# Linear attention and its borders: weight splits behind two borders, value rows between key decays, key turns before the row wait, half of the scaling on ScalarE

## The chip, the cores and the metric

The kernel runs on one core of a Trainium2 chip. The metric is the device time of one execution in microseconds (us); lower is better.

## What is computed

Two transformer blocks in float32 on 512 tokens of width 1024. The first (dilated attention, a convolution, a mixture of 32 experts) is untouched. The second prepends 16 meta tokens (528 rows) and computes

```
proj = rmsnorm(h) @ w_in            # stick-breaking q,k,v; linear q,k,v; gate rows g_r; gate rank g_lr; merge gates
sb   = stick_breaking(sb_q, sb_k, sb_v)                       # 8 heads of 64
glog = log_sigmoid(g_lr @ w_gk_up + b_gk) / 16
# gated linear attention, 4 heads, keys of 128, values of 256:
S_t  = diag(exp(glog_t)) S_{t-1} + k_t^T v_t ;  o_t = q_t S_t
o    = rmsnorm(o, gla_head_norm) * silu(g_r)
mix  = (sigmoid(m_sb) * (sb @ w_sb_out) + sigmoid(m_gla) * (o @ w_gla_out)) @ w_o
h    = h + rmsnorm(mix)
ffn  = (gelu(dwconv(rmsnorm(h) @ w_up)) * (rmsnorm(h) @ w_gate)) @ w_down
h    = h + rmsnorm(ffn)
```

## The kernel before, in words

Each stage is a block of its own, written out by hand for each engine with semaphores between them; at the end of a block all engines meet at a barrier. The order of the work on each engine is the order of the code. The stages that matter here are stick_breaking (until 1058 us), gated_linear (until 1251), mix_and_project (until 1518) and feed_forward.

**Weights in two parts.** A product of float32 is made of three products of fp32r parts (function three, L1670 to L1672). So each weight piece of 128 x 1024 is split: ScalarE copies it into a high part (Parts.high, L1561), VectorE subtracts that from the raw values to give the low part (Parts.low, L1569), and TensorE waits for the low one (Parts.use). There are four places for split pieces and three for raw chunks; the DMA queue loads chunk c when the last piece of chunk c - 3 has its low part (Parts.load_until, L1525). Pieces are numbered and split in order: low_ok and high_ok count them. GK_AT + 2 is piece 19, the third key head of the linear attention; the next block's first pieces are split in the block before. UP_AT + 2 and UP_AT + 3 are the second column tile's pieces of the feed-forward.

**gated_linear.** First the gate rank (two products, pieces LR_AT), whose results ScalarE takes (L2376), then eight small products with the gate's weights (L2279) into three PSUM banks in turn, each freed by a take; then keys. Then the seven levels of a binary scheme for the attention inside a chunk (L2297), with products of value rows between them: 20 of them (four column blocks by five row tiles), 24 matmuls each, again three banks. A row tile 4 (the 16 meta rows) is the last that reads a column block's weights, and behind its take ScalarE splits the pieces that take their places. After the last level VectorE decays the queries (L2509), ScalarE computes the key decays in 4 heads x 5 spans (L2415), VectorE multiplies the keys (L2511).

**The chunk loop.** Five chunks: the 16 meta tokens and four of 128. In each, TensorE turns the decayed keys (4 transposes, L2334), waits for the state and for the rows of the chunk before, forms the outputs (L2342 and L2344: attention times values, queries times state, banks 1 and 2), the new state's product (L2349), and one product of gate rows (bank 7); then it waits for the normed rows and turns them (8 transposes, L2365). ScalarE takes the keys (L2429), sums four heads' squares (L2434), takes the root (L2437), the gate rows (L2440), splits a piece in odd chunks, and takes the turned rows (L2424). VectorE updates the state (L2524), forms the variance (L2531), its inverse (L2533), and scales four heads from PSUM into rows (L2537).

**mix_and_project** ends with the second norm, whose rows are turned (L2681), taken by ScalarE (L2769) and given low parts by VectorE (L2854).

Of the kernel before, what the change touches and what calls it, by code (L numbers as in the profile page):

```python
# [14 lines left out]
P = 128  # L15
# [1837 lines left out]
def stick_breaking(g):  # L1853
# [27 lines left out]
    with ExitStack() as cx:  # L1881
# [132 lines left out]
        @block.scalar  # L2014
        def _(act):
            def take_projection(n):
                first, m, half = outputs[n]
                act.wait_ge(ready, n + 1)
                bank = psum[:, BANKS[n % 8], :]
                lo, width = columns_of(first, half)  # L2020
                for r in range(2):
                    src, h = bank[HD * r:HD * r + HD, :], 2 * m + r
                    if first == Q_AT:
                        for d in range(2):
                            last = act.activation(q2[HD * d:HD * d + HD, h, lo:lo + width], src[:, 0:width], ACT.Copy, scale=HD ** -0.5)
                    elif half == 0:
                        act.activation(k2[h][HD:, 0:META], src[:, 0:META], ACT.Copy)
                        last = act.activation(k2[h][0:HD, 0:2 * P], src[:, META:LATER_KEYS], ACT.Copy)
                    else:
                        last = act.activation(k2[h][HD:, META:], src[:, 0:2 * P], ACT.Copy)  # L2030
                last.then_inc(taken, 1)
                if half == 1:
                    parts.high(act, first + m + W_SLOTS)

            def take_rows(r):
                c, t = row_outputs[r]
                n = len(outputs) + r
                act.wait_ge(ready, n + 1)
                if t == TT:
                    act.wait_ge(zeroed, 1)  # L2040
                rows = P if t < TT else META
                act.activation(v[0:rows, t, c * 256:(c + 1) * 256], psum[0:rows, row_bank(n), 0:256], ACT.Copy).then_inc(taken, 1)

            for n in range(len(outputs)):
                take_projection(n)
            step = Steps(act, astep)

            def log_term(h):

                act.wait_ge(z_sb, 6 * h + 6)  # L2050
                if h >= 2:
                    act.wait_ge(w_ok, 2 * (h - 1))
                z, t = zbuf[:, h % 3, :], sbuf[:, h % 2, :]
                step(act.activation(t, z, ACT.Abs))
                step(act.activation(t, t, ACT.Exp, scale=-1.0))
                act.activation(t, t, ACT.Ln, bias=1.0).then_inc(soft, 1)

            def weights(h):
                z, t = zbuf[:, h % 3, :], sbuf[:, h % 2, :]
                act.wait_ge(arg_ok, 6 * h + 4)  # L2060
                act.activation(z[:, 0:Z_META], t[:, 0:Z_META], ACT.Exp).then_inc(w_ok, 1)
                act.wait_ge(arg_ok, 6 * h + 6)
                act.activation(z[0:META, Z_META:], t[0:META, Z_META:], ACT.Exp).then_inc(w_ok, 1)

            def take(h):
                lo = 64 * (h % 2)
                act.wait_ge(pv_ps, 3 * h + 2)
                act.activation(sbT[lo:lo + 64, h // 2, META:], psum[0:HD, 5, :], ACT.Copy).then_inc(pv_sb, 1)
                act.wait_ge(pv_ps, 3 * h + 3)
                act.wait_ge(q_ps, h + 1)  # L2070
                act.activation(sbT[lo:lo + 64, h // 2, 0:META], psum[0:HD, 6, 0:META], ACT.Copy).then_inc(pv_sb, 1)
                act.activation(gq[:, h // 2, (h % 2) * HALF:(h % 2 + 1) * HALF], psum[:, 6, META:META + HALF], ACT.Copy,
                               scale=DK ** -0.5).then_inc(q_sb, 1)

            act.wait_ge(zeroed, 2)
            log_term(0)
            take_rows(0)
            take_rows(1)
            log_term(1)
            for r in range(2, TT + 1):  # L2080
                take_rows(r)
            parts.high(act, GQ_AT)
            take_rows(TT + 1)
            parts.high(act, GQ_AT + 1)
            for r in range(TT + 2, 2 * (TT + 1)):
                take_rows(r)
            parts.high(act, GQ_AT + 2)
            parts.high(act, GQ_AT + 3)
            for h in range(HEADS):
                weights(h)  # L2090
                if h + 2 < HEADS:
                    log_term(h + 2)
                take(h)
                if h % 2:
                    parts.high(act, GQ_AT + h // 2 + W_SLOTS)

        @block.vector
        def _(dve):
# [74 lines left out]
                elif h % 2 == 0:  # L2173
                    parts.low(dve, GQ_AT + h // 2 - 1 + W_SLOTS)
            add_other_keys(HEADS - 1)
            parts.low(dve, GK_AT + 2)

        @block.sync
        def _(sp):
# [4 lines left out]
def gated_linear(g):  # L2184
# [55 lines left out]
    with ExitStack() as cx:  # L2240
# [9 lines left out]
        o_ps, s_ps, s_ok = sem("out_in_psum"), sem("state_in_psum"), sem("state_ready")  # L2250
        sq, var, root = sem("out_squares"), sem("out_variance"), sem("out_root")
        rows_ok, oT_ps, oT_ok = sem("out_rows_ready"), sem("oT_in_psum"), sem("oT_ready")
        block = cx.enter_context(nc.Block())

        @block.gpsimd
# [9 lines left out]
        def _(pe):  # L2265
# [60 lines left out]
            pe.wait_ge(lv_ok, LEVELS + 1)  # L2326

            pe.wait_ge(dec, 1)
            for c, (c0, n) in enumerate(span):
                vt = v[0:n, (c - 1) % (TT + 1), :]  # L2330
                for h in range(GH):
                    if c and h == 0:
                        pe.wait_ge(kd_sb, c)
                    last = pe.transpose(psum[0:n, 0, h * P:(h + 1) * P], k[:, h, c0:c0 + n], ident)  # L2334
                last.then_inc(kd_ps, 1)
                if c:
                    pe.wait_ge(s_ok, 2 * c)
                    pe.wait_ge(rows_ok, c)
                for h in range(GH):
                    at_ = attm[:, h, :] if c == 0 else att[:, h, c0 - META:c0 - META + P]  # L2340
                    dst = psum[0:n, 1 + h // 2, (h % 2) * DV:(h % 2 + 1) * DV]
# [15 lines left out]
                turned(pe, psum[:, 7, 0:width], w, x, lo, width).then_inc(gr_ps, 1)  # L2357
                if c % 2:
                    parts.read_by(GR_AT + c // 2, gr_ps, c + 1)
                pe.wait_ge(rows_ok, c + 1)  # L2360
                for half in range(2):
                    if c:
                        pe.wait_ge(oT_ok, 2 * (c - 1) + half + 1)
# [6 lines left out]
        def _(act):  # L2370
# [7 lines left out]
            half = lambda x, h, i: x[:, h, i * HALF:(i + 1) * HALF]  # L2378
            for i in range(2):
                take(LR + i, lrT[:, i * HALF:(i + 1) * HALF], 16, HALF)  # L2380
            parts.high(act, LR_AT + W_SLOTS)
            act.wait_ge(nb_ok, 1)
            for h in range(GH):
# [12 lines left out]
            def take_value_rows(r):  # L2396
                c, t = row_outputs[r]
                rows_ = P if t < TT else META
                take(ROWS + r, v[0:rows_, t, c * 256:(c + 1) * 256], rows_, 256)
                if t == TT:  # L2400
                    parts.high(act, GV_AT + 2 * c + W_SLOTS)
                    parts.high(act, GV_AT + 2 * c + 1 + W_SLOTS)

            for n in range(LEVELS):
                act.wait_ge(diff, n + 1)
                act.activation(level_part(e, n), level_part(e, n), ACT.Exp, scale=1.0 / 16).then_inc(e_ok, 1)
                take_value_rows(2 * n)
                take_value_rows(2 * n + 1)

            act.wait_ge(qk_ok, LEVELS)  # L2410
            act.activation(flat(e), flat(cs), ACT.Exp, scale=-1.0 / 16).then_inc(qd_e, 1)
# [1 line left out]
            for h in range(GH):  # L2413
                for c, (c0, n) in enumerate(span):
                    last = act.activation(e[:, h, c0:c0 + n], cs[:, h, c0:c0 + n], ACT.Exp, scale=1.0 / 16, bias=nlast[:, h, c:c + 1])  # L2415
            last.then_inc(kd_e, 1)
            for r in range(2 * LEVELS, len(row_outputs)):
                take_value_rows(r)

            def take_oT(c):  # L2420
                c0, n = span[c]
# [5 lines left out]
            for c, (c0, n) in enumerate(span):  # L2427
# [7 lines left out]
                                   accum_out=ss[0:n, h:h + 1]).then_inc(sq, 1)  # L2435
                act.wait_ge(var, c + 1)
                act.activation(rstd[0:n, :], rstd[0:n, :], ACT.Sqrt).then_inc(root, 1)  # L2437
                act.wait_ge(gr_ps, c + 1)
                width = UP_PARTS[c % 2][1]
                act.activation(gr[:, c, 0:width], psum[:, 7, 0:width], ACT.Copy).then_inc(gr_sb, 1)  # L2440
# [5 lines left out]
        def _(dve):  # L2446
# [5 lines left out]
            for l in range(LEVELS):  # L2452
# [2 lines left out]
                step(dve.scalar_tensor_tensor(out=masks[:, l, :], in0=xor, scalar=1.0, in1=g["before"], op0=ALU.is_equal,  # L2455
                                              op1=ALU.mult))
            dve.engine_nop().then_inc(masks_ok, 1)
            parts.low(dve, LR_AT + W_SLOTS)

            dve.wait_ge(soft, 1)  # L2460
# [54 lines left out]
            for c, (c0, n) in enumerate(span):  # L2515
# [11 lines left out]
                        last.then_inc(s_ok, 1)  # L2527
                dve.wait_ge(sq, 4 * c + 4)
                if c:
                    dve.wait_ge(root, c)  # L2530
                dve.tensor_scalar(rstd[0:n, :], ss[0:n, :], 1.0 / DV, EPS, ALU.mult, ALU.add).then_inc(var, 1)  # L2531
                dve.wait_ge(root, c + 1)
                step(dve.reciprocal(rstd[0:n, :], rstd[0:n, :]))  # L2533
                if c:
                    dve.wait_ge(oT_ps, 2 * c)
                for h in range(GH):
                    last = dve.tensor_scalar(rows[0:n, h * DV:(h + 1) * DV], psum[0:n, 1 + h // 2, (h % 2) * DV:(h % 2 + 1) * DV],  # L2537
                                             rstd[0:n, h:h + 1], None, ALU.mult)
                last.then_inc(rows_ok, 1)
# [55 lines left out]
def mix_and_project(g):  # L2595
# [24 lines left out]
    with ExitStack() as cx:  # L2620
# [167 lines left out]
        def _(dve):  # L2788
# [67 lines left out]
            for t in range(TT + 1):  # L2856
# [5 lines left out]
                    parts.low(dve, UP_AT + 1)  # L2862
                if t:
                    low_rows(t - 1)
            parts.low(dve, UP_AT + 2)
            parts.low(dve, UP_AT + 3)
            low_rows(TT)

        @block.sync
        def _(sp):  # L2870
            sp.dma_start(gain, a["norm_mix_post_2"].to_broadcast([P, D])).then_inc(loads, 16)
            sp.dma_start(gpre, a["norm_ffn_pre_2"].to_broadcast([P, D])).then_inc(loads, 16)
            sp.dma_start(g["meta"][0:HISTORY, :], a["meta_tokens_2"][META - HISTORY:, :]).then_inc(loads, 16)
            parts.load_until(sp, 42)
    parts.new_phase()


def feed_forward(g):
# [15 lines left out]
    with ExitStack() as cx:  # L2894
# [96 lines left out]
        def _(dve):  # L2991
# [12 lines left out]
            def product(m):  # L3004
                dve.wait_ge(act_ok, m + 1)
                dve.wait_ge(ready, 3 * m + 3)
                dve.tensor_tensor(products[m], y[:, m % 2, :], psum[:, BANKS[(3 * m + 2) % 6], :], ALU.mult).then_inc(prod_ok, 1)  # L3007

            for m in range(FM):
                conv(m)  # L3010
                if m:
# [50 lines left out]
```

## Time and profile before

| | |
|---|---|
| time, median of 3 runs | 1889.44 us (1889.11 to 1890.83) |
| profiled execution, span from first to last instruction | 1896.1 us |
| TensorE (PE) busy | 1746.9 us, 92% |
| VectorE (DVE) busy | 799.2 us, 42% |
| ScalarE (ACT) busy | 587.5 us, 31% |
| mean granted TensorE clock | 0.972 of 2.4 GHz |
| DMA | 355.38 MB, mean 187 GB/s |

The span belongs to one execution and is 6.7 us longer than the median of the runs. Matmuls are pipelined, so the records of neighbouring ones overlap; an idle time of PE is counted from the end of the last record.

### The profile page before, as it was taken

To read this page: it belongs to the slowest core of one execution; us is meant where nothing else is said; L and a number is where in the kernel's file an instruction comes from. 1 tells how busy PE (TensorE), PEld (TensorE's weight loads), DVE (VectorE), ACT (ScalarE), POOL (GpSimd) and SP (SyncE) were. 2 spreads that over 40 slices of the span, in tenths; PEclk is the share of its full clock that TensorE was granted. 3 is DMA by queue.
4 is the path that set the end of the run, shared out by engine and by line. 5 is a ranking of instruction groups with operands and counts; after the bars stand their busy time and mean duration, and the time that the engine had idled before them with its cause. 6 is when DMAs were issued, how large, how long until landed. Compare 5 with 4: busy or idle time off the path is not lost. (4 is left out here: it accounts for less than half of the span.)

```text
span 1896.1 us, 27345 instructions
## 1 busy us (share of the span) xinstructions
PE 1746.9 (92%) x11698; PEld 1351.5 (71%) x11698; DVE 799.2 (42%) x1348; ACT 587.5 (31%) x992; POOL 61.3 (3%) x86
## 2 busy tenths in 40 slices
PE   6999989999989889938999899899999999999997
PEld 2883445666555556528965799789998789999886
DVE  3864556221111111144377567342246544444333
ACT  4333422100000000036677433443223423322322
POOL 1001000000000000020000000000000000000000
PEclk9999989999999999978999899999999999999999
DMA  9855623899999999971210111122223033223221
GB/s 370 272 184 163 263 104 137 334 427 426 426 428 428 426 426 427 426 281 51 76 36 9 46 45 45 45 87 92 90 90 111 1 113 99 89 89 99 103 88 45
DMA packets 111217, 355.38 MB, mean 187 GB/s; under 512 B 8663, under 2 KB 71405, under 8 KB 97399
## 3 DMA queue, kind: packets, MB, share of 16 engines
q1 hardware_dynamic: 106342, 343.89, 47.2%
q0 software_dynamic: 4224, 9.33, 1.4%
q8 instruction: 94, 1.54, 0.3%
q10 hardware_dynamic: 530, 0.40, 0.1%
q14 instruction: 27, 0.22, 0.0%
HBM read 330.21 MB, written 23.33 MB: 186 GB/s over the span
## 5 line engine op out<-in xcount | busy, mean ns | idle before, releaser
L1670 PE MATMUL psum<-parts_memory 128*128 128x256 f32 (+3 forms) x1136 | 347.3, 306 | 14.7 <-issue 4.7
L1671 PE MATMUL psum<-parts_memory 128*128 128x256 f32 (+3 forms) x1136 | 344.1, 303 | 0.0
L1672 PE MATMUL psum<-parts_memory 128*128 128x256 f32 (+3 forms) x1136 | 343.3, 302 | 0.0
L1569 DVE TENSOR_TENSOR parts_memory<-fixed,parts_memory 128x1024 fp32r<-128x1024 f32 x139 | 167.1, 1222 | 206.6 <-ACT parts_memory L1561 206.3
L1670 PEld LDWEIGHTS psum<-parts_memory 128*128 128x128 f32 x1136 | 218.8, 193 | 24.6 <-issue 8.1
L1672 PEld LDWEIGHTS psum<-parts_memory 128*128 128x128 f32 x1136 | 218.7, 193 | 6.9
L1671 PEld LDWEIGHTS psum<-parts_memory 128*128 128x128 f32 x1136 | 218.6, 192 | 6.9
L1670 PE MATMUL psum<-mix_parts,parts_memory 128*128 128x256 f32 (+2 forms) x664 | 206.4, 311 | 4.7 <-PEq L2620 4.0
L1671 PE MATMUL psum<-mix_parts,parts_memory 128*128 128x256 f32 (+2 forms) x664 | 207.4, 312 | 0.0
L1672 PE MATMUL psum<-mix_parts,parts_memory 128*128 128x256 f32 (+2 forms) x664 | 206.4, 311 | 0.0
L1561 ACT ACTIVATE parts_memory<-fixed 128x1024 fp32r<-128x1024 f32 x139 | 143.2, 1055 | 123.9 <-PE psum L1672 109.7
L1329 PE MATMUL psum<-fixed,first_block_memory 128*64 128x256 f32 x1216 | 138.0, 380 | 16.7 <-DMA fixed<-in_w_exp_up_dram 14.7
L1329 PEld LDWEIGHTS psum<-fixed,first_block_memory 128*64 128x64 f32 x1216 | 94.8, 137 | 65.2 <-issue 34.1
L1670 PEld LDWEIGHTS psum<-mix_parts,parts_memory 128*128 128x128 f32 x664 | 126.2, 190 | 12.6 <-issue 4.2
L1672 PEld LDWEIGHTS psum<-mix_parts,parts_memory 128*128 128x128 f32 x664 | 126.4, 190 | 7.0
L1671 PEld LDWEIGHTS psum<-mix_parts,parts_memory 128*128 128x128 f32 x664 | 125.9, 190 | 7.4
L1329 PE MATMUL psum<-attention_memory,first_block_memory 128*64 128x256 f32 x896 | 101.8, 380 | 13.7 <-DMA attention_memory<-in_w_exp_up_dram 11.0
L1329 PEld LDWEIGHTS psum<-attention_memory,first_block_memory 128*64 128x64 f32 x896 | 70.2, 137 | 49.5 <-issue 27.4
L1450 DVE TENSOR_TENSOR first_block_memory<-first_block_memory,psum 128x256 f32<-128x256 f32 x33 | 13.9, 422 | 216.2 <-PE psum L1329 216.2
L1395 ACT ACTIVATE first_block_memory<-psum 128x512 f32<-128x512 f32 x36 | 21.5, 596 | 223.6 <-PE psum L1313 223.6
L1313 PE MATMUL psum<-parts_memory 128*128 128x256 f32 x576 | 85.9, 294 | 1.4 <-DVE parts_memory L1433 1.4
L1313 PEld LDWEIGHTS psum<-parts_memory 128*128 128x128 f32 x576 | 72.6, 190 | 16.8 <-issue 12.3
(412 smaller groups left out, 2365.1 us busy)
## 6 DMA issues: line engine op xcount, KB each, us to landing
fixed<-in_w_exp_gate_dram SPq DMA_DIRECT2D x19, 2048.0 KB, 29.7
fixed<-in_w_exp_up_dram SPq DMA_DIRECT2D x19, 2048.0 KB, 30.9
fixed<-in_w_exp_down_dram SPq DMA_DIRECT2D x19, 2048.0 KB, 31.7
fixed<-in_w_in_dram SPq DMA_DIRECT2D x36, 1024.0 KB, 5.1
attention_memory<-in_w_exp_up_dram SPq DMA_DIRECT2D x14, 2048.0 KB, 31.0
attention_memory<-in_w_exp_down_dram SPq DMA_DIRECT2D x14, 2048.0 KB, 31.2
attention_memory<-in_w_exp_gate_dram SPq DMA_DIRECT2D x14, 2048.0 KB, 29.5
fixed<-in_w_mod_dram SPq DMA_DIRECT2D x8, 2048.0 KB, 8.8
```

The lines of the kernel that those rows point to most:

```text
L1313: last = pe.matmul(psum[:, bank, part * BC:part * BC + BC], h2P[:, i, t, (2 * u + part) * P:(2 * u + part + 1) * P], pick[:, t, :], start= ...
L1329: last = pe.matmul(psum[half(h), bank, 0:256], x[:, k, :], w[:, k, 256 * h:256 * h + 256], start=(k == 0), stop=(k == KT - 1))
L1395: act.activation(xT[:, i, 2 * u:2 * u + 2, :], psum[:, BX + u % 2, :].rearrange("p (k n) -> p k n", k=2), ACT.Copy).then_inc(xt_ok, 1)
L1450: dve.tensor_tensor(h, h, strided(psum[:, BU, 0:256], 4), ALU.mult).then_inc(h_ok, 1)
L1561: act.activation(out, raw, ACT.Copy).then_inc(self.high_ok, 1)
L1569: dve.tensor_tensor(out, raw, high.bitcast(F32), ALU.subtract).then_inc(self.low_ok, 1)
L1670: pe.matmul(out, x(0), w(0), start=start, stop=False)
L1671: pe.matmul(out, x(0), w(1), start=False, stop=False)
L1672: return pe.matmul(out, x(1), w(0), start=False, stop=stop)
```

## The change

- In stick_breaking the split of piece GK_AT + 2 is dropped, and made in gated_linear: its high part behind the two gate-rank takes, its low part behind the masks.
- The takes of value rows 14, 15 and 16 stand between the key decays of the heads; the splits that followed the takes come after all decays.
- In the chunk loop, the keys of chunk c + 1 are turned behind the gate rows of chunk c and before the wait for its rows. The wait for the rows ahead of the outputs goes, as the row turns have waited for them already.
- Heads 2 and 3 are scaled by ScalarE (semaphores out_inverse_root and out_rows_of_scalar_ready), heads 0 and 1 by VectorE.
- The low parts of UP_AT + 2 and UP_AT + 3 are made at the start of feed_forward; their high parts stay where they were. Two weight chunks that wait for them are issued there too.

```diff
@@ stick_breaking, scalar and vector
-                if h % 2:
+                if h % 2 and h + 1 < HEADS:
                     parts.high(act, GQ_AT + h // 2 + W_SLOTS)
             add_other_keys(HEADS - 1)
-            parts.low(dve, GK_AT + 2)
@@ gated_linear, tensor
+            def turn_keys(c):
+                c0, n = span[c]
+                if c:
+                    pe.wait_ge(kd_sb, c)
+                for h in range(GH):
+                    last = pe.transpose(psum[0:n, 0, h * P:(h + 1) * P], k[:, h, c0:c0 + n], ident)
+                last.then_inc(kd_ps, 1)
+
+            turn_keys(0)
             for c, (c0, n) in enumerate(span):
-                for h in range(GH):
-                    if c and h == 0:
-                        pe.wait_ge(kd_sb, c)
-                    last = pe.transpose(psum[0:n, 0, h * P:(h + 1) * P], k[:, h, c0:c0 + n], ident)
-                last.then_inc(kd_ps, 1)
                 if c:
                     pe.wait_ge(s_ok, 2 * c)
-                    pe.wait_ge(rows_ok, c)
...
+                if c < TT:
+                    turn_keys(c + 1)
                 pe.wait_ge(rows_ok, c + 1)
+                pe.wait_ge(rows_act, c + 1)
@@ gated_linear, scalar
                 take(LR + i, lrT[:, i * HALF:(i + 1) * HALF], 16, HALF)
+            parts.high(act, GK_AT + 2)
             parts.high(act, LR_AT + W_SLOTS)
...
                     last = act.activation(e[:, h, c0:c0 + n], cs[:, h, c0:c0 + n], ACT.Exp, scale=1.0 / 16, bias=nlast[:, h, c:c + 1])
+                if h < GH - 1:
+                    take_value_rows(2 * LEVELS + h)
             last.then_inc(kd_e, 1)
             for r in range(2 * LEVELS, len(row_outputs)):
-                take_value_rows(r)
+                if r >= 2 * LEVELS + GH - 1:
+                    take_value_rows(r)
+                if r >= 2 * LEVELS + GH - 2:
+                    for q in range(2 * LEVELS if r == 2 * LEVELS + GH - 2 else r, r + 1):
+                        split_after(q)
...
                 act.activation(rstd[0:n, :], rstd[0:n, :], ACT.Sqrt).then_inc(root, 1)
+                if c:
+                    act.wait_ge(oT_ps, 2 * c)
+                act.wait_ge(inverse, c + 1)
+                for h in range(GH - BY_ACT, GH):
+                    last = act.activation(rows[0:n, h * DV:(h + 1) * DV], psum[0:n, 1 + h // 2, (h % 2) * DV:(h % 2 + 1) * DV],
+                                          ACT.Copy, scale=rstd[0:n, h:h + 1])
+                last.then_inc(rows_act, 1)
@@ gated_linear, vector
+            parts.low(dve, GK_AT + 2)
             parts.low(dve, LR_AT + W_SLOTS)
...
-                    dve.wait_ge(root, c)
+                    dve.wait_ge(rows_act, c)
...
-                step(dve.reciprocal(rstd[0:n, :], rstd[0:n, :]))
+                dve.reciprocal(rstd[0:n, :], rstd[0:n, :]).then_inc(inverse, 1)
+                dve.wait_ge(inverse, c + 1)
...
-                for h in range(GH):
+                for h in range(GH - BY_ACT):
@@ mix_and_project, vector and sync
-            parts.low(dve, UP_AT + 2)
-            parts.low(dve, UP_AT + 3)
             low_rows(TT)
-            parts.load_until(sp, 42)
+            parts.load_until(sp, 40)
@@ feed_forward, vector
+            parts.low(dve, UP_AT + 2)
+            parts.low(dve, UP_AT + 3)
             for m in range(FM):
```

## Rows read from the trace of the kernel before

**Rows 1.** The page's first part: busy time, share of the span, instructions.

```profile
PE 1746.9 (92%) x11698; PEld 1351.5 (71%) x11698; DVE 799.2 (42%) x1348; ACT 587.5 (31%) x992; POOL 61.3 (3%) x86
```

**Rows 2.** TensorE's waits from 1200 to 1300 us: in total, times, longest.

```profile
PE psum L2365 <- DVE fixed L2537: 5.0, 4, 1.6
PE psum L1670 <- PEq L2240: 1.0, 1, 1.0
```

**Rows 3.** Timeline, border behind stick_breaking: start, duration, engine, what, [idle before <- releaser].

```profile
1055.19 0.69 DVE L2128 TENSOR_TENSOR fixed<-fixed,psum 64x512 f32<-64x512 f32 x1 [5.68 <-ACT fixed L2071]
...
1056.55 1.23 DVE L1569 TENSOR_TENSOR parts_memory<-fixed,parts_memory 128x1024 fp32r<-128x1024 f32 x1 [0.67 <-ACT parts_memory L1561]
...
1058.10 0.56 PE L1670 MATMUL psum<-parts_memory 128*128 128x264 f32 x1 [3.60 <-PEq L1881]
```

**Rows 4.** Timeline, ScalarE's split and the eight small gate products.

```profile
1066.91 1.04 ACT L1561 ACTIVATE parts_memory<-fixed 128x1024 fp32r<-128x1024 f32 x1
1067.06 4.26 PE L2279 MATMUL psum<-linear_memory 16*128 16x264 f32 x16 [0.47 <-ACT linear_memory L2376]
```

**Rows 5.** Timeline, key decays, the value row that waits, decayed keys, first key turns.

```profile
1182.19 5.58 ACT L2415 ACTIVATE linear_memory<-linear_memory,fixed 128x16 f32<-128x16 f32 x20 [7.21 <-DVE fixed L2509]
...
1187.80 2.36 DVE L2511 TENSOR_TENSOR linear_memory<-linear_memory 128x2112 f32<-128x2112 f32 x1 [5.64 <-ACT linear_memory L2415]
...
1188.09 0.39 PE L1670 MATMUL psum<-parts_memory 128*128 128x256 f32 x1 [2.74 <-ACT linear_memory L2376]
...
1197.35 0.60 PE L2334 MATMUL psum<-fixed,linear_memory 128*16 128x128 f32 x4 [0.46 <-ACT linear_memory L2376]
```

**Rows 6.** Timeline, a middle chunk of the loop.

```profile
1214.34 1.66 DVE L2524 SCALAR_TENSOR_TENSOR linear_memory<-linear_memory,fixed,psum 128x256 f32<-128x256 f32 x4 [7.59 <-PE psum L2349]
...
1216.57 1.66 DVE L2537 TENSOR_SCALAR fixed<-psum,fixed 128x256 f32<-128x256 f32 x4
...
1217.17 0.38 ACT L2440 ACTIVATE fixed<-psum 128x256 f32<-128x256 f32 x1 [0.85 <-PE psum L1672]
...
1218.28 1.09 PE L2365 MATMUL psum<-fixed 128*128 128x128 f32 x8 [1.14 <-DVE fixed L2537]
...
1219.21 0.60 PE L2334 MATMUL psum<-fixed,linear_memory 128*128 128x128 f32 x4
1219.65 0.60 PE L2342 MATMUL psum<-linear_memory 128*128 128x256 f32 x2
```

**Rows 7.** Timeline, the row turns of the last chunk.

```profile
1249.09 1.09 PE L2365 MATMUL psum<-fixed 128*128 128x128 f32 x8 [1.58 <-DVE fixed L2537]
```

**Rows 8.** Timeline, border behind mix_and_project.

```profile
1513.67 1.09 PE L2681 MATMUL psum<-fixed,mix_memory 128*128 128x128 f32 x8 [1.34 <-DVE mix_memory L2846]
1514.37 1.09 ACT L2769 ACTIVATE mix_parts<-psum 128x512 fp32r<-128x512 f32 x2 [1.29 <-PE psum L2681]
1514.73 2.35 DVE L1569 TENSOR_TENSOR parts_memory<-fixed,parts_memory 128x1024 fp32r<-128x1024 f32 x2
...
1517.00 1.28 DVE L2854 TENSOR_TENSOR mix_parts<-psum,mix_parts 128x512 fp32r<-128x512 f32 x2
...
1518.75 0.55 PE L1670 MATMUL psum<-mix_parts,parts_memory 128*128 128x256 f32 x1 [3.99 <-PEq L2620]
```

**Rows 9.** Windows: stretch, length, busy per engine; PEclk 1.00 is 2.4 GHz.

```profile
1186.37:1189.78 3.41, 1.69 (x14) 1.70 (x15) 1.98 (x1) 3.41 (x9) 0.00 (x0) 1.00 0.00 0
1247.81:1251.22 3.41, 1.14 (x9) 0.94 (x9) 2.35 (x5) 1.29 (x4) 0.00 (x0) 1.00 0.00 0
1251.22:1254.63 3.41, 3.41 (x16) 3.41 (x17) 1.66 (x5) 3.15 (x7) 0.00 (x0) 0.50 1.02 321
1517.46:1524.28 6.82, 5.53 (x26) 5.56 (x27) 0.82 (x2) 0.42 (x2) 0.00 (x0) 0.50 1.05 351
1056.66:1063.48 6.82, 5.38 (x24) 5.41 (x25) 5.76 (x15) 0.00 (x0) 2.42 (x4) 0.50 0.01 5
```

**Rows 10.** Windows: the chunk loop behind chunk 0's low clock.

```profile
1206.84:1250.18 43.34, 38.36 (x249) 34.86 (x248) 15.00 (x38) 18.38 (x56) 0.00 (x0) 1.00 0.00 1
```

More of the change, by code:

```diff
@@ L2252, in gated_linear @@
         rows_ok, oT_ps, oT_ok = sem("out_rows_ready"), sem("oT_in_psum"), sem("oT_ready")
+        rows_act, inverse = sem("out_rows_of_scalar_ready"), sem("out_inverse_root")
+        BY_ACT = 2
         block = cx.enter_context(nc.Block())
@@ L2399, in take_value_rows, with split_after @@
                 take(ROWS + r, v[0:rows_, t, c * 256:(c + 1) * 256], rows_, 256)
+            def split_after(r):
+                c, t = row_outputs[r]
                 if t == TT:
@@ L2406, in _ @@
                 act.activation(level_part(e, n), level_part(e, n), ACT.Exp, scale=1.0 / 16).then_inc(e_ok, 1)
-                take_value_rows(2 * n)
-                take_value_rows(2 * n + 1)
+                for r in (2 * n, 2 * n + 1):
+                    take_value_rows(r)
+                    split_after(r)
             act.wait_ge(qk_ok, LEVELS)
@@ L2415, in _ @@
                     last = act.activation(e[:, h, c0:c0 + n], cs[:, h, c0:c0 + n], ACT.Exp, scale=1.0 / 16, bias=nlast[:, h, c:c + 1])
+                if h < GH - 1:
+                    take_value_rows(2 * LEVELS + h)
             last.then_inc(kd_e, 1)
             for r in range(2 * LEVELS, len(row_outputs)):
-                take_value_rows(r)
+                if r >= 2 * LEVELS + GH - 1:
+                    take_value_rows(r)
+                if r >= 2 * LEVELS + GH - 2:
+                    for q in range(2 * LEVELS if r == 2 * LEVELS + GH - 2 else r, r + 1):
+                        split_after(q)
             def take_oT(c):
```

## The prediction

> **What bounds the kernel now.** I read the page first: TensorE is busy for 92% of the span [rows 1], the chain that ended last names its products and almost no wait, so the kernel goes at TensorE's pace and a change is worth what it takes out of TensorE's idle time or gives back of its clock. The list of TensorE's waits, taken over the linear attention, shows the wait of the row turns for VectorE: 5.0 us in four pieces [rows 2]. The timelines around the edits show four more places:
>
> - the border from stick-breaking to linear attention: TensorE starts at 1058.10 after 3.60 us idle. VectorE's add ends at 1055.88; what still runs is a weight split of ScalarE and then of VectorE, up to 1057.78. No one in that block reads it [rows 3];
> - the value rows: 2.74 us, ended by a take of ScalarE's that stood behind twenty key decays, 5.58 us from 1182.19 [rows 5];
> - the border from linear attention to mixing: 1.58 us before the last row turns [rows 7] and 1.0 behind them [rows 2];
> - the border from mixing to feed-forward: TensorE has stopped at 1514.76 (1513.67 and 1.09), VectorE makes two lows from 1514.73 to 1517.08 and only then the last token rows' low halves, to 1518.28; TensorE starts at 1518.75, 3.99 us [rows 8].
>
> The windows of the granted clock show that it fell to half (1.2 GHz) at or near three of these borders, and stayed at 2.4 GHz at the 2.74 us wait [rows 9].
>
> **Part by part.** The sum is made in the profiled execution, span 1896.1 us. The runs shown have a median of 1889.44 us, 6.7 us less; I subtract the same microseconds from the median.
>
> *First border.* High and low of piece 19 go behind the border. The barrier then waits for VectorE's add at 1055.88 in place of 1057.78: 1.90 us less idle [rows 3]. The DMA queue waits for nothing new, since the chunks issued in that block need earlier lows. What moves: ScalarE now makes two splits where it made one, between the gate-rank takes and the eight gate takes. One costs 1.04 us [rows 4]. TensorE can run three of its eight small products into free banks: the eight take 4.26 us, some 0.5 each, so about 1.5 us from 1067.06, to 1068.6. The first take, which frees a bank, starts when the split ends, at 1067.95; with a second one it would start at 1068.9 to 1069.0 and last some 0.4 (0.38 for such a take in [rows 6]). So TensorE loses 0.7 to 1.04; I take 0.9. The weights themselves are wanted only two products later, and VectorE's extra low lies beside these (1.23 in [rows 3]); if that cover were gone it would cost that. Net 1.0.
>
> *Value rows.* Three takes move between the key decays. The decays of a head last 5.58 / 4 = 1.40 us, so the first take comes at about 1183.6, and TensorE, which comes to its next product at 1185.35 (1188.09 less 2.74), finds its bank. The 2.74 us go [rows 5]. Three takes of 0.4 put the decayed keys 1.2 us later; VectorE then needs 2.36 us for them and is done near 1191.3, while TensorE has value rows until about 1194.2 (the key turns at 1197.35, less 0.46 idle and less 2.7). Hidden, with 2.8 us to spare. The last weights' highs still follow the last take, as before. Gain 2.7.
>
> *Chunk loop.* Before, in a middle chunk: the state update ends at 1216.00, then variance, root, inverse, then four scalings 1216.57 to 1218.23; the gate rows end at 1217.14 (1218.28 less 1.14); row turns 1218.28; key turns 1219.21; outputs 1219.65 [rows 6]. After, VectorE scales two heads, 0.83 us, to 1217.40. No row shows ScalarE reading PSUM with a column as scale; the nearest is its take of the gate rows, 0.38 us for the same 128x256 [rows 6]. Two make 0.76, to 1217.3. Bounds: 0 beyond VectorE's half, or 0.83 each (twice the take and VectorE's time doubled), to 1218.23, which is no gain; I take the row's 0.38. TensorE turns the next keys from 1217.14 for 0.44 (start of the outputs less start of the turns) to 1217.58: by then the rows are ready. The 1.14 us wait is filled, and the next chunk starts without key turns. Three chunks: 3.4. The last chunk has no keys to turn; its 1.58 us wait [rows 7] shrinks by two scalings, 0.83. Chunk 0 has no wait there and moves only the order. Behind ScalarE's two scalings stand the take of the gate rows, a split in odd chunks (1.05), the oT takes and the key take; the scalings fit into 0.85 us that it idles before the gate rows [rows 6]. If they didn't, the key take is next to be late, and the state products. Gain 4.2.
>
> *Last border.* The lows of UP_AT + 2 and + 3 go into the next block; the last rows' lows start when ScalarE's second half lets them: its take starts at 1514.37, VectorE about 0.6 later (as it is free at 1514.8), and ends near 1516.3. The barrier's 0.47 (1518.28 to 1518.75) stays: TensorE starts at 1516.75, 2.0 us earlier [rows 8]. The loads of two weight chunks wait for these lows and go with them, some 2 us later and behind the next block's load of its gain; they are not split before the second column tile. TensorE wants the moved lows for that tile too, two products (some 8 us, by 5.53 us of work in the 6.8 us behind 1517.46 [rows 9]) after its start; two lows take 2.35, so they are there by 1519.2. Gain 2.0.
>
> Idle time together: 1.0 + 2.7 + 4.2 + 2.0 = 9.9 us.
>
> *The clock.* TensorE was at half rate for 5.38 us of its work behind the first border, 3.41 behind the second, 5.53 behind the last [rows 9]; at full rate these would cost half: 2.7, 1.7 and 2.8 us. Before the falls it had idled 3.60 in one piece, 1.58 and 0.99 around the row turns, and 3.99 [rows 2, 3, 7, 8]. Afterwards the idle pieces are 1.7, then 0.75 and 1.0, then 1.34 and 2.0 around 1.09 of turns [rows 8]. The first two are no more idle than the stretch of the value rows that kept its clock with 1.69 busy in 3.41 us. The third isn't: I let it fall and recover sooner, 1.1 of 2.8. In this execution that is 2.7 + 1.7 + 1.1 = 5.5. Bounds 0 and 7.2. Where the falls sit against the work differs between executions, so I take 4.0.
>
> One rule speaks to this. The clock fell at 1251.22 after a stretch with 1.14 us of work in it and no idle piece over 1.6 us [rows 9]. The Trainium skill, TensorE: Matmul & The Clock Gate, section "Why this matters for your kernels", advises no idle gap over about 3 us between bursts, as if shorter ones were safe; by it alone all three borders would keep their speed, which is the rival of full speed below. The trace disagrees with it, unless the row turns count as idle.
>
> **Sum.** 9.9 + 4.0 = 13.9: 1889.4 - 13.9 = 1875.5 us. A difference of 3.8 us (0.2%) is about what a measurement of this kernel can tell from no change.
>
> **Rivals.**
> 1. *Full speed at every border.* 9.9 + 7.2 = 17.1 gives 1872.3. For: two of three idle pieces are halved. Against: the fall at 1251.22. Chance 0.15.
> 2. *The clock gives nothing back*, because it falls on the shorter gaps as well: 1879.5. For: 1.58 and 0.99 were enough once. Against: 1.69 of work in 3.41 was not. 0.18.
> 3. *ScalarE's half is late*: the scalings take up to 0.83 each, or the key take behind them slips. The row wait shrinks only by the key turns: 3 x 0.44 in place of 4.2, 2.9 lost: 1878.4. For: ScalarE also carries a split in odd chunks. Against: 0.85 idle just there. 0.15.
> 4. *The waits are handed on.* Some other engine ends the two blocks last (ScalarE or the queue), and the value rows' 2.74 turn into a wait for the decayed keys. Left are the 4.2, less the 0.9 in ScalarE's queue: 1886.1. For: 0.47 of the last barrier isn't VectorE's. Against: every other end in rows 3 and 8 is earlier. 0.07.
> 5. *Slower: the clock stays low through the chunk loop.* Chunk 0 enters it at half speed already, and more turns stand together now. The loop's 43.3 us at full clock [rows 10] would cost up to 21.7 more: 1897.3. It decides from 28 us of work at half speed (13.9 twice); with 15 us or less the kernel is still over 6 faster. Against: with idle pieces in it the loop held full clock. 0.03.
>
> My forecast has the other 0.42. Faster by over 0.2% (under 1885.7): the forecast, rivals 1 to 3, 0.90; within 0.2%, rival 4, 0.07; slower 0.03. Range: from below full speed, 1871, to a late ScalarE without clock, 1879.5 + 2.9 = 1882.5. The likeliest alone: 1873.5 to 1877.5.
>
> **What would show it.** TensorE's idle before L1670 about 1.7 at the first border and 2.0 at the last; no wait of over 0.3 before the row turns of the middle chunks and about 0.75 in the last; no 2.7 before the value rows; the middle chunks over 1 us closer together; small gate products some 0.9 longer. The clock's falls behind the first two borders gone. The span near 1882. It is wrong if ScalarE's scalings take over 0.6 each, if a new wait for keys_ready stands before the state products, or if half-speed stretches turn up elsewhere.

## The result and the profile after

The changed kernel took 1881.66 us in the median of four runs (1879.37 to 1883.22), the kernel before 1890.13 in four runs beside it (1889.11 to 1892.60). The ratio is 0.9943, 95% interval 0.9926 to 0.9960: 10.8 us faster, from 7.6 to 14. It is an estimate of its own and not the quotient of the two medians, which lie 8.5 us apart. Both are given below where they differ. The forecast was 13.9 us faster and 1875.5, range 1871.0 to 1882.5; the median lies in the range, near its upper end. Two more series of the same kernel on other occasions gave 0.9919 and 0.9945, medians 12.8 and 13.1 us apart (below).

The profiled executions differ by more, spans 1896.1 and 1877.3. The stage windows of the changed kernel show where; they are cut at the end of the last product of stick-breaking, the first small gate product, the first level product, the first output product, the last row turn, and the last turn of the second norm. Columns: stretch, length, busy time of TensorE, its weight loads, VectorE, ScalarE, GpSimd, then the granted clock, the DMA share and GB/s.

```profile
1052.37:1060.64 8.27, 6.10 (x49) 5.92 (x49) 6.38 (x19) 1.86 (x6) 2.43 (x4) 1.00 0.02 4
1060.64:1092.53 31.89, 30.75 (x208) 28.90 (x209) 17.57 (x34) 18.38 (x26) 0.00 (x0) 0.89 0.22 67
1092.53:1189.40 96.87, 93.47 (x780) 89.51 (x780) 64.69 (x74) 36.78 (x57) 0.00 (x0) 1.00 0.11 34
1189.40:1235.81 46.41, 45.53 (x281) 40.37 (x280) 16.60 (x38) 26.99 (x79) 0.00 (x0) 0.96 0.14 45
1235.81:1498.86 263.05, 257.57 (x1937) 245.81 (x1936) 115.88 (x193) 95.50 (x180) 0.00 (x0) 1.00 0.26 85
1498.86:1877.28 378.42, 363.64 (x2089) 320.36 (x2088) 162.00 (x201) 110.34 (x174) 0.00 (x0) 0.99 0.28 91
```

The same six windows of the kernel before:

```profile
1054.50:1067.06 12.56, 8.49 (x49) 8.31 (x49) 9.04 (x25) 2.81 (x7) 2.42 (x4) 0.73 0.01 3
1067.06:1098.02 30.96, 30.48 (x208) 28.91 (x208) 15.01 (x27) 17.49 (x25) 0.00 (x0) 0.89 0.21 69
1098.02:1197.88 99.86, 93.72 (x780) 89.55 (x780) 64.70 (x74) 36.98 (x57) 0.00 (x0) 1.00 0.13 43
1197.88:1250.17 52.29, 47.31 (x281) 41.48 (x280) 20.53 (x48) 23.51 (x69) 0.00 (x0) 0.93 0.07 21
1250.17:1514.76 264.59, 259.11 (x1937) 247.35 (x1936) 116.02 (x194) 95.65 (x180) 0.00 (x0) 0.99 0.26 84
1514.76:1896.10 381.34, 364.55 (x2089) 321.31 (x2088) 161.87 (x201) 110.36 (x174) 0.00 (x0) 0.98 0.27 90
```

Line by line the change is -4.29, +0.93, -2.99, -5.88, -1.54, -2.92: 16.7 us. The other 2.1 of the 18.8 lie ahead of the first edit, where the code is the same (1054.50 against 1052.37). So two traces can differ by a few us there without any edit. Over all 13 traces of this case the first cut lies between 1048.00 and 1055.45 us, always behind the same code, and TensorE's clock was at half for 51 us ahead of it in the earliest and for 72 us in the latest: this is where much of the scatter of the spans comes from. The time from the first cut to the end is the better measure of an edit: 841.6 and 841.4 us in two traces of the kernel before, 824.9, 825.0 and 825.6 in three of the changed one.

In TensorE's waits of the changed kernel the 2.7 before the value rows and the row waits of the middle chunks are gone; these are the waits of 1040 to 1190 and of 1190 to 1300:

```profile
PE psum L1670 <- PEq L1881: 1.7, 1, 1.7
...
PE psum L2280 <- ACT fixed L2383: 0.7, 1, 0.7
...
PE psum L1670 <- PEq L2239: 1.0, 1, 1.0
PE psum L2372 <- DVE fixed L2564: 0.9, 1, 0.9
```

The timeline of a middle chunk, beside [rows 6]:

```profile
1206.49 0.88 DVE L2564 TENSOR_SCALAR fixed<-psum,fixed 128x256 f32<-128x256 f32 x2
1206.55 0.84 ACT L2460 ACTIVATE fixed<-psum,fixed 128x256 f32<-128x256 f32 x2 [0.31 <-DVE fixed L2559]
1206.88 0.60 PE L2335 MATMUL psum<-fixed,linear_memory 128*128 128x128 f32 x4
1207.27 0.39 ACT L2465 ACTIVATE fixed<-psum 128x256 f32<-128x256 f32 x1
1207.48 1.06 PE L2372 MATMUL psum<-fixed 128*128 128x128 f32 x8
...
1216.44 0.60 PE L2335 MATMUL psum<-fixed,linear_memory 128*128 128x128 f32 x4
```

ScalarE and VectorE scale two heads each side by side and end within 0.02 us of each other, at 1207.38. The key turns run meanwhile, and the row turns start at 1207.48 with no idle time ahead. The key turns of neighbouring chunks start 9.56 us apart (1206.88 to 1216.44); before it was 10.7.

The first border and the small gate products, beside [rows 3] and [rows 4]:

```profile
1054.07 0.36 PE L1670 MATMUL psum<-parts_memory 128*128 128x264 f32 x1 [1.71 <-PEq L1881]
...
1060.49 1.99 ACT L1561 ACTIVATE parts_memory<-fixed 128x1024 fp32r<-128x1024 f32 x2
...
1060.64 1.60 PE L2280 MATMUL psum<-linear_memory 16*128 16x264 f32 x6 [0.47 <-ACT linear_memory L2383]
...
1062.39 2.62 ACT L2383 ACTIVATE fixed<-psum,fixed 128x264 f32<-128x264 f32 x6
1062.90 3.13 PE L2280 MATMUL psum<-linear_memory 16*128 16x264 f32 x10 [0.66 <-ACT fixed L2383]
```

TensorE makes three products (six instructions), then waits 0.66 us for the take that stands behind two splits.

The last border, beside [rows 8]: the low halves start at 1499.09, TensorE at 1500.85, and the two moved lows lie behind it.

```profile
1499.09 1.29 DVE L2881 TENSOR_TENSOR mix_parts<-psum,mix_parts 128x512 fp32r<-128x512 f32 x2 [0.18 <-ACT mix_parts L2796]
...
1500.70 1.23 DVE L1569 TENSOR_TENSOR parts_memory<-fixed,parts_memory 128x1024 fp32r<-128x1024 f32 x1 [0.32 <-PEq L2647]
...
1500.85 0.35 PE L1670 MATMUL psum<-mix_parts,parts_memory 128*128 128x256 f32 x1 [1.99 <-PEq L2647]
```

### The profile page after: what moved, and what is told of

It is laid out like the page before. It is cut to its first block and busy times, and to the rows that moved or that the text cites. A ratio compares the mean times of both kernels' runs of the same rounds, so it can differ in the third digit from the quotient of the medians.

```text
span 1877.3 us, 27345 instructions
## 1 busy us (share of the span) xinstructions
PE 1741.2 (93%) x11698; PEld 1346.3 (72%) x11698; DVE 794.9 (42%) x1338; ACT 590.3 (31%) x1002; POOL 60.4 (3%) x86
## 3 DMA queue, kind: packets, MB, share of 16 engines
q8 instruction: 94, 1.54, 0.3%
## 5 line engine op out<-in xcount | busy, mean ns | idle before, releaser
L1670 PEld LDWEIGHTS psum<-parts_memory 128*128 128x128 f32 x1136 | 216.5, 191 | 19.4 <-issue 10.8
L1450 DVE TENSOR_TENSOR first_block_memory<-first_block_memory,psum 128x256 f32<-128x256 f32 x33 | 13.9, 422 | 214.6 <-PE psum L1329 214.6
L1313 PEld LDWEIGHTS psum<-parts_memory 128*128 128x128 f32 x576 | 72.6, 190 | 16.7 <-issue 12.3
```

The lines of the kernel that those rows point to most:

```text
L1313: last = pe.matmul(psum[:, bank, part * BC:part * BC + BC], h2P[:, i, t, (2 * u + part) * P:(2 * u + part + 1) * P], pick[:, t, :], start= ...
L1450: dve.tensor_tensor(h, h, strided(psum[:, BU, 0:256], 4), ALU.mult).then_inc(h_ok, 1)
L1670: pe.matmul(out, x(0), w(0), start=start, stop=False)
```

## The experiments

The idle terms can be read off; open were the clock's share, and why the timed runs showed 8.5 us between medians where the traces showed 18.8. Where a text below names a half-speed stretch, it is one in which the granted clock was 0.50, that is 1.2 GHz.

**1. The kernel before, unchanged.**

> The kernel before, unchanged, profiled once more and timed. Theory 1 (the profiled execution of before was a slow one, with more half-speed stretches around the edits than most): the new span lies near 1888 us, and at least one of the falls of the granted clock at the borders behind stick-breaking, linear attention and mixing is missing, shorter, or elsewhere. Theory 2 (those falls belong to every execution of before, and the change's clock gain was lost again elsewhere): span 1894 to 1897 with the same three falls, and the timed runs still 6 us shorter.

Ratio 1.0001 (0.9992 to 1.0010). On this occasion the unchanged kernel had a median of 1893.16 us in 33 runs that spread from 1887.69 to 1898.05: a median of four can be off by some us. The new span is 1891.3. Its stages before and behind the value rows:

```profile
1049.83:1061.52 11.69, 7.62 (x48) 7.44 (x49) 8.96 (x25) 2.81 (x7) 2.42 (x4) 0.85 0.01 4
...
1090.90:1192.28 101.38, 95.24 (x781) 91.06 (x781) 64.71 (x74) 36.97 (x57) 0.00 (x0) 0.98 0.14 42
```

Here the clock's low stretch behind the first border was shorter (11.69 against 12.56 us), but it fell at the 2.7 us wait of the value rows, where the first trace had none (101.38 against 99.86). From the first cut to the end both traces take the same, 841.4 and 841.6 us; they differ ahead of it, 1049.8 against 1054.5. Neither theory fits fully: the falls do move between executions, as theory 1 says, yet from the first cut on the first trace was not a slow one; its slow part was upstream. In both traces the kernel before loses to the clock at some of its waits, and not at the same ones.

**2. The first border's edit alone.**

```diff
-                if h % 2:
+                if h % 2 and h + 1 < HEADS:
                     parts.high(act, GQ_AT + h // 2 + W_SLOTS)
...
-            parts.low(dve, GK_AT + 2)        # stick_breaking
+            parts.high(act, GK_AT + 2)       # gated_linear, behind the gate-rank takes
+            parts.low(dve, GK_AT + 2)        # gated_linear, behind the masks
```

> Only the split of piece 19 moved behind the first border. Both theories: TensorE idles 1.7 us there instead of 3.6, the eight small gate products lose 0.7 to 1.0, net idle gain 1.0. Theory 1 (clock gives on average nothing much): 0 to 2 us faster. Theory 2 (the clock no longer falls behind this border, 2.7 us each time): 3 to 4 us faster.

Ratio 0.9997 (0.9986 to 1.0007): 0.6 us, from 2.6 faster to 1.3 slower. In the trace the wait at the border is 1.7 us and the small gate products wait 0.7 for a take. The clock did not fall at the border, but it fell at the untouched value-row wait. That agrees with theory 1; theory 2's 3 to 4 us lie outside the interval.

**3. The value rows' edit alone.**

```diff
                     last = act.activation(e[:, h, c0:c0 + n], cs[:, h, c0:c0 + n], ACT.Exp, scale=1.0 / 16, bias=nlast[:, h, c:c + 1])
+                if h < GH - 1:
+                    take_value_rows(2 * LEVELS + h)
...
```

> Only the three takes of value rows moved between the key decays. Both theories: the 2.74 us wait of TensorE disappears and the key turns start 2.7 to 3.0 us earlier against the last level, 2.7 us faster. Rival: a new wait for the decayed keys stands before the key turns and takes over 1 us of it back.

Ratio 0.9987 (0.9976 to 0.9998), 2.5 us. The stage of the levels takes 96.85 us, as in the changed kernel (96.87), against 99.86 and 101.38 before. No wait for the decayed keys took its place; the rival falls.

**4. The last border's edit alone.**

```diff
-            parts.low(dve, UP_AT + 2)        # mix_and_project
-            parts.low(dve, UP_AT + 3)
...
-            parts.load_until(sp, 42)
+            parts.load_until(sp, 40)
...
+            parts.low(dve, UP_AT + 2)        # feed_forward
+            parts.low(dve, UP_AT + 3)
             for m in range(FM):
```

> Only the two lows moved behind the border to the feed-forward. Both theories: TensorE idles 2.0 us there instead of 4.0. Theory 1: the clock still falls behind the border in most executions (the row turns with their gaps are enough), 2.0 us faster, up to 3. Theory 2: the clock stays up, 4 to 5 us faster. Rival: the second column tile of the feed-forward waits for the moved loads or lows, and there is no gain.

Ratio 0.9989 (0.9979 to 1.0000), 2.1 us. The last stretch takes 378.20 us against 381.34 and 381.03 before, 3 us less. The clock still fell behind the border, but for 3.41 us in place of 6.83:

```profile
1517.74:1521.15 3.41, 3.02 (x14) 3.06 (x15) 2.36 (x2) 0.39 (x1) 0.00 (x0) 0.50 0.50 169
1521.15:1524.57 3.42, 3.42 (x31) 3.42 (x31) 1.48 (x3) 1.34 (x2) 0.00 (x0) 1.00 1.01 334
```

That is theory 1: 2.0 of idle time and up to one more. The moved loads and lows cost nothing that the stretch shows.

**5. The changed kernel again, and 6. the chunk loop's two edits alone.**

> The changed kernel unchanged, timed in more runs. Theory 1 (the gain is the idle time taken out, 9.9 us, plus a clock gain of a few us that shows only over many executions): 10 to 14 us under the kernel before. Theory 2 (the clock gives nothing on average): 8.5 to 10 us. If the first comparison's 8.5 us between medians was mostly luck of four runs each, the ratio here lies under 0.9945.

Ratio 0.9919 (0.9899 to 0.9939), 11.5 to 19 us faster; the medians, 1879.57 and 1892.36, are 12.8 apart, which is theory 1's size. Theory 2's 8.5 to 10 lie below the interval. The trace takes 825.0 us from the first cut on, with the same falls as the first one.

```diff
-                    pe.wait_ge(rows_ok, c)            # ahead of the outputs
...
+                if c < TT:
+                    turn_keys(c + 1)
                 pe.wait_ge(rows_ok, c + 1)
+                pe.wait_ge(rows_act, c + 1)
...
+                for h in range(GH - BY_ACT, GH):      # ScalarE
+                    last = act.activation(rows[...], psum[...], ACT.Copy, scale=rstd[0:n, h:h + 1])
...
-                for h in range(GH):                   # VectorE
+                for h in range(GH - BY_ACT):
```

> Only the chunk loop's two edits, keys turned ahead and half of the scaling on ScalarE. Theory 1: the middle chunks lose their 1.1 us wait and get 1.1 to 1.3 us shorter each, the last wait goes from 1.6 to about 0.8; 4.2 to 4.7 us faster, and up to 1 more where the clock stays up at the border behind. Rival: ScalarE's scalings are late or push the key take back, the gain is 1.3 us.

Ratio 0.9985 (0.9976 to 0.9994), 2.8 us. In the trace the loop takes 48.07 us against 52.29, with the same half-speed stretch in chunk 0: 4.2 us, the forecast's term. The timed interval (1.1 to 4.5) includes it. The clock did not fall at the border behind the loop either: the stretch to the next cut takes 263.06 us against 264.59.

**7. Keys turned ahead, all scaling on VectorE.** The edit is the TensorE part of the diff above (turn_keys moved, the wait ahead of the outputs gone), without the wait for rows_act.

> Only the keys turned ahead of the row wait, all four scalings on VectorE. TensorE's wait before the row turns falls from 1.14 to about 0.7 in the middle chunks (0.44 of turns fill it), and stays 1.6 in the last. The chunks come 0.44 us closer together each. Rival: the wait stays 1.1, because the chain through VectorE starts with the outputs and not with the turns, so that the whole chunk moves up: also 0.44 each, but with other waits.

One execution, span 1891.0, with no timed series. The row turns wait:

```profile
1215.47 1.09 PE L2370 MATMUL psum<-fixed 128*128 128x128 f32 x8 [0.73 <-DVE fixed L2542]
1225.72 1.09 PE L2370 MATMUL psum<-fixed 128*128 128x128 f32 x8 [0.67 <-DVE fixed L2542]
1235.97 1.09 PE L2370 MATMUL psum<-fixed 128*128 128x128 f32 x8 [0.69 <-DVE fixed L2542]
1244.97 0.33 PE L2370 MATMUL psum<-fixed 128*128 128x128 f32 x1 [1.57 <-DVE fixed L2542]
```

0.7 in the middle chunks and 1.57 in the last, and 10.25 us from chunk to chunk, 0.44 less than 10.69. The loop takes 50.99 us. So of its 4.2 us the key turns give 1.3 and ScalarE's half 2.9: the latter takes some 0.7 more in each middle chunk and 0.7 in the last. One thing speaks against the prediction's reasoning on the clock: the waits around the last row turns are as long as before (1.57 and 0.99), and yet the clock stayed at 2.4 GHz behind them in this trace, where it fell in the five other traces with these waits.

```profile
1247.05:1253.88 6.83, 6.83 (x58) 6.83 (x59) 4.66 (x12) 6.52 (x15) 0.00 (x0) 1.00 0.96 308
```

**8. The changed kernel without the first border's edit.** Experiment 2's diff taken back.

> The changed kernel with the split of piece 19 back in the stick-breaking block. The single parts, timed alone, add up to 8.0 us, the whole to 12.8 to 15.3. Theory 1 (the parts are additive, the difference is noise of the timed runs): this is slower than the whole by the 3.4 us that the first border's two stages gained net in the trace (4.3 less 0.9), and the chunk loop stays at 46.4 us with 3.4 us of half clock. Theory 2 (the first edit also sets where the clock's falls sit against the later work): the chunk loop is back at 48.1 us with 6.8 us of half clock, and the whole difference is about 5 us.

Ratio 0.9942 (0.9921 to 0.9964), median 1881.81 against 1881.58 for the changed kernel on the same occasion: no difference that the timed runs can tell, though with some 4 us to either side on each they can't rule out 3.4 us. The first two stages, in its windows:

```profile
1054.92:1065.09 10.17, 6.10 (x49) 5.92 (x49) 7.61 (x20) 2.81 (x7) 2.43 (x4) 1.00 0.01 3
1065.09:1096.18 31.09, 30.61 (x209) 28.68 (x209) 16.43 (x33) 17.48 (x25) 0.00 (x0) 0.89 0.22 69
```

With 3.6 us of idle time the clock this time stayed up at the border. The two stages take 41.26 us against 40.16 in the changed kernel: with the clock alike in both, the edit gives 1.90 and costs 0.80. Theory 2 falls: the chunk loop stays at 46.4 us, so the shorter low stretch there isn't this edit's doing. Theory 1 has the loop right and not the 3.4 us: in this trace, from the first cut to the end, it is 0.5 us slower (825.4 against 824.9).

**9. The changed kernel once more.**

> The changed kernel once more, as the partner of the next one on the same chip: 12 to 16 us under the kernel before, and a span with the same falls of the clock behind the first gate products, in chunk 0 and behind the last border.

Ratio 0.9945 (0.9924 to 0.9965), 6.6 to 14 us faster; by the ratio 10.4 us, less than the 12 to 16 that I expected, by the medians (1881.58 and 1894.63) 13.1, within them. Span 1877.7; the falls are where the first trace of it has them, with one more, of 3.4 us, in the mixing stage (264.0 us instead of 263.05).

**10 and 11. Both splits behind the eight gate takes.** The improved version, run on two occasions:

```diff
                 take(LR + i, lrT[:, i * HALF:(i + 1) * HALF], 16, HALF)
-            parts.high(act, GK_AT + 2)
-            parts.high(act, LR_AT + W_SLOTS)
             act.wait_ge(nb_ok, 1)
             for h in range(GH):
                 for i in range(2):
                     take(LR + 2 + 2 * h + i, half(qe, h, i), P, HALF, scale=-1.0, func=ACT.Identity, bias=nbias[:, h:h + 1])
+            parts.high(act, GK_AT + 2)
+            parts.high(act, LR_AT + W_SLOTS)
```

> The changed kernel with both of ScalarE's splits moved behind the eight gate takes. If the 0.7 to 1.1 us that the small gate products lost come from the second split ahead of their takes, the wait before L2280 goes, the stage gets 0.7 to 1.1 us shorter than in the changed kernel and the time falls by as much. Rival: the products are slow by the half clock alone, and nothing changes; or the low parts come late and the third key head waits.

> The changed kernel with ScalarE's two splits behind the eight gate takes, again. If the 2.5 us that the stage of the gate products gained in the first trace (31.9 to 29.4) hold, this is 2 to 3 us faster than the changed kernel on the same chip. If only the 0.7 us wait belongs to the edit and the rest was the place of the clock's fall in one execution, under 1.5 us.

Ratios to the kernel before 0.9911 (0.9896 to 0.9926) and 0.9911 (0.9890 to 0.9931), medians 1876.63 and 1876.80, where the changed kernel had 1879.57 and 1881.58. ScalarE's takes now follow the products at once, and the splits come behind:

```profile
1060.38 0.38 ACT L2383 ACTIVATE linear_memory<-psum 16x264 f32<-16x264 f32 x1 [2.53 <-PE psum L1672]
1061.62 3.54 ACT L2383 ACTIVATE fixed<-psum,fixed 128x264 f32<-128x264 f32 x8 [0.86 <-PE psum L2280]
1065.06 2.00 ACT L1561 ACTIVATE parts_memory<-fixed 128x1024 fp32r<-128x1024 f32 x2
```

The window of that stage, the first of the two traces:

```profile
1060.82:1090.23 29.41, 28.93 (x208) 27.68 (x208) 17.50 (x34) 18.22 (x26) 0.00 (x0) 0.94 0.19 59
```

29.41 us in both traces against 31.89, 31.88 and 31.92 in three of the changed kernel: 0.7 is the wait, the rest a half-speed stretch that is 3.4 us long instead of 6.8. Whether the edit shortens that stretch isn't shown: in the second trace of the kernel before it is 3.4 us as well (29.38 us for the stage, with one split ahead of the takes). The third key head does not wait. The first expectation had the wait right and missed the size, 2.5 us in place of 0.7 to 1.1; in the second the stage's 2.5 held. From the first cut on the two traces take 822.0 and 822.3 us, some 3 less than those of the changed kernel. By the medians the timed runs are 2.9 and 4.8 us faster than the changed kernel's; the intervals of the ratios overlap with that one's, so the timed runs alone don't settle it.

## Why the prediction was right, and where it was off

- **First border, net 1.0.** Right: 1.90 less idle, 0.80 to 0.93 lost by the small gate products. Experiments 8 and 10 show both sides. The loss was avoidable: with the splits behind the takes nothing waited for them.
- **Value rows, 2.7.** 3.0 in the trace. The recorded wait leaves out the overlap of neighbouring matmuls: in an unbroken row records of 0.28 us start 0.12 apart, and the one behind the wait took 0.39. That is the missing 0.3.
- **Chunk loop, 4.2.** Right to 0.1. The price taken for ScalarE's scaling, 0.38 each from its take, was a little low: two last 0.84 where a sum of two takes is 0.76 and two pipelined ones less. It sits beside VectorE's 0.88 (I took 0.83), so nothing followed. Experiment 7 separates the two edits: 1.3 and 2.9.
- **Last border, 2.0.** Right: 3.99 became 1.99; the moved loads and lows were never waited for.
- **The clock, 4.0.** This is the term that was mis-sized. With the idle terms as measured (1.0 + 3.0 + 4.2 + 2.0 = 10.2) the first comparison leaves nothing for it by the medians and 0.6 by the ratio; the second series leaves 2.6 and 5.1, the third 2.9 and 0.2. In the first pair of traces it was 6.5 (16.7 less 10.2): 2.4 at the first border, 1.5 behind the linear attention, 0.9 at the last border, and 1.7 in chunk 0, which I hadn't forecast. That part, 52.29 to 46.41 less the loop's 4.2, shows in every trace with both the value rows' and the loop's edits and in none with one of them. Why is open; a kernel with those two alone wasn't run. The forecast priced the falls of one trace and scaled them down by a guess; the table below shows what the other traces say.
- **The row and the rule.** The clock fell behind idle pieces of under 2 us each, at the second border of the kernel before (1.58 and 0.99) and at the last border of the changed one (1.34 and 1.99), and it stayed up through 3.60 us in two traces (experiments 7 and 8). The Trainium skill, in TensorE: Matmul & The Clock Gate, section "Why this matters for your kernels", advises no gap over about 3 us; as a line between falls and no falls that disagrees with these traces on both sides.
- **Rivals.** Full speed at every border: the last border fell in each trace. ScalarE late: refuted by 0.84 beside 0.88. Waits handed on: no such wait, save the 0.66 that was priced. Slow chunk loop: its clock is 0.96 against 0.93 before. No clock gain: not excluded by the timed intervals of the first and third series, excluded by that of the second (11.5 to 19) and by the traces. The price of rival 5 was wrong: at half clock TensorE's 38.4 us of work in those 43.3 [rows 10] would take up to 38.4 us more, and not 21.7.
- **Luck.** The range was met with 0.8 us to spare, and not for the reason that its upper end was set for: ScalarE was not late. The forecast stood on a base of three runs, 1889.44, and the kernel before had medians of 1893.16, 1892.36 and 1894.63 on later occasions. As a difference, 13.9 lies above the first ratio's 10.8 and the third's 10.4 and below the second's 15.3.

The half-speed stretches behind each place, in the 13 traces, sorted by the wait that stands there:

| place | with the wait of before | with it shortened or gone |
|---|---|---|
| first border, 3.60 us or 1.71 | 6.8 us in three traces, 3.4 in two, none in two | none in six |
| value rows, 2.74 or none | 3.4 in three, none in three | none in seven |
| behind the linear attention, 1.58 or 0.86 | 3.4 in five, none in one | none in seven |
| last border, 3.99 or 1.99 | 6.8 in six | 3.4 in seven |

With the edits the falls were gone at three places and shorter at the last in every trace; without them three of the four came only in some executions. The value rows' fall, which the forecast put at nothing, belongs in the sum. An estimate from these counts and the stage lengths (2.4 us lost to a stretch of 6.8 us at the first border, 1.5 to each of 3.4, and 0.9 at the last border) is 1.5 + 0.8 + 1.3 + 0.9 = 4.5 us on average, and 6.2 with chunk 0's 1.7. The traces, averaged, give 6.1 (841.5 less 825.2, less 10.2). The timed series give less, and why is open.

The single parts, timed alone, give 0.6 + 2.5 + 2.1 + 2.8 = 8.0 us, the whole 10.4 to 15.3. Each of the four intervals is 2 us wide to either side, so this alone says little. From the first cut on, the traces give 0.8 + 3.3 + 2.0 + 7.0 = 13.1 for the parts and 16.3 for the whole. The half-speed stretches from the first cut to the one behind the last border, included, add up to 30.7 us in both traces of the kernel before and in those of the first border's, the value rows' and the last border's edit alone, to 23.9 with the loop's alone, and to 13.7, 13.7 and 17.1 with all four. With one wait removed the clock fell as long at other places. That is one trace for each part; that it holds for most executions is argued and not shown.

## What to carry to other kernels

Before a barrier, look which engine ends last and whether anyone on this side reads its last result: 1.9 and 2.0 us lay in splits that only the next block read. When such work is moved, put it behind what another engine is waiting for on the far side as well; a second split ahead of the eight takes cost 0.8 us, and both behind them nothing. A term for the clock belongs in a forecast as a range and not as its value in one trace: where it falls moves the total by several us between executions of one kernel. So count the falls in several traces before you price them, and judge small edits by many runs or by stage windows that start at the first edit.

## What the runs showed of the hardware

The unchanged kernel spread over 10 us in 33 runs (1887.69 to 1898.05). Over 13 traces the same code ahead of the first edit ended between 1048.00 us, with 51 us of it at half clock, and 1055.45, with 72. TensorE's clock was at half for 6.8 or 3.4 us behind the same border, or not at all, in different executions: with 3.6 us idle the stage took 12.56, 11.69 and 10.17 us. After the 1.71 us that the edit left it did not fall in six traces. ScalarE scaled 128x256 from PSUM with a column as scale in 0.42 us each, in a pair, while VectorE read another bank in 0.44; VectorE alone took 1.66 for four, 0.415 each, so side by side it lost 0.025 each at most.
